# A fused two-model kernel on one core: the modulation summed by VectorE in the last feed-forward, bias lines made in layer 0, two norms in one pass

## The chip, the cores and the metric

The kernel runs on one core of a Trainium2 chip. A core has five engines that run their own instruction streams and meet by semaphores: TensorE (matmuls, results in PSUM), VectorE, ScalarE, GpSimd, and SyncE, which issues the DMAs here. The metric is the device time in microseconds of one execution of the whole program.

## The reference

```python
def first_block(x, ...):                      # DEPTH = 2, S = 512, D = 1024, all float32
    for l in range(DEPTH):
        h = rms_norm(x, norm1[l]); proj = h @ w_in[l]
        ...                                   # four kinds of attention of four heads each
        x = x + mixed @ w_out[l]
        h2 = rms_norm(x, norm2[l])
        x = x + jnp.square(jax.nn.relu(h2 @ w_up[l])) @ w_down[l]
    return rms_norm(x, final_norm)

def second_block(x, c, norm_g, w_ada, b_ada, w_in, ..., rel_bias, final_g):
    mod = c @ w_ada[0] + b_ada[0]             # c: 1 x 1024, w_ada: 1024 x 3072
    shift, scale, gate = jnp.split(mod, 3, axis=-1)
    h = rmsnorm(x, norm_g[0]) * (1.0 + scale[:, None]) + shift[:, None]
    proj = h @ w_in[0]                        # 1024 x 8192
    ...                                       # bias = rel_bias[bucket of the distance], 24 heads
    outs = [dilated_window_attention(q, k, v, dil, win // dil, bias_g) for three groups of eight heads]
    ...                                       # merge of the groups, a pooling branch, gates
    x = x + gate[:, None] * (merged @ w_out[0])
    return rmsnorm(x, final_g)
```

The output of first_block is the input x of second_block. A norm divides each row by the root of its mean square plus 1e-6 and multiplies by a gain.

## The kernel before

X (512 rows as four tiles of 128, 1024 columns) stays in SBUF. A float32 product is made of three passes: each operand is split into a high part, which TensorE multiplies exactly, and a low part, and L1637, L1638 and L1639 (the helper `three`) multiply high by high, high by low and low by high. A product of 512 columns is a *job*: four PSUM banks, G, one for each row tile, in two halves of 512 rows of weights each, so 96 matmuls, which are all of one half before those of the other. Each half's weights are a *piece*: SP loads it into one of four slots of `raw`, ScalarE copies it to `w_hi` (L1144 in the first model, L525 in the second), and GpSimd subtracts in two instructions to `w_lo` (L1107). w_hi and w_lo have two slots, so a piece can be split as soon as the half two before it is done. All engines work strictly in the order in which their streams are written; nothing but that order and the semaphores decides.

A layer has six projection jobs (index, A, C, B, D, V), the index scores with a search for the top keys, the attention, two output jobs and the feed-forward: four groups, each with two jobs up and two down. In a group VectorE squares and splits the hidden rows (L1620 to L1622), and for each bank of a down job adds to X (L1603), which frees the bank. These groups are a hardware loop on every engine. The norm of the feed-forward is not applied before it but as a factor of this addition.

The second block begins with a stage of its own (`second_scalar`, `second_vector`, `second_tensor`, from L525, L614 and L845). TensorE computes the modulation in six dense jobs: the 1 x 1024 vector c, spread over 128 rows as cb_hi and cb_lo, times 512 columns of w_ada each. All 128 rows of each result are the same. VectorE takes the rows to h_full (L641), TensorE turns them into columns, and VectorE adds b_ada (L651). In the same loop TensorE makes 24 bias lines (one for each head: the one-hot table `hot` of distances times a head's row of rel_bias, L874), which ScalarE stores 128 rows wide in `stage` (L536). They go to memory in one 4.6 MB store, from which skewed loads make the bias tiles. Meanwhile the first model's last norm is applied to X (squares L1152, root L1157, rows L633), the second model's norm is then taken of the new X in the same way (L1152, L1376), the rows are turned, scaled and shifted (L560) and split (L668, L669), and the first product of w_in_2 starts once all eight column tiles are split.

## Time and profile before

| | us |
|---|---|
| median of 3 runs | 2209.36 |
| lowest and highest run | 2195.4, 2210.68 |
| the profiled execution | 2206.09 |
| its span, first to last instruction | 2204.1 |
| busy: TensorE, VectorE, ScalarE, GpSimd | 1976.2, 957.9, 666.0, 798.4 |

The profile is of one execution. Its mean granted TensorE clock was 0.932 of full speed. In the rows below, PE is TensorE, PEld its weight loads, DVE VectorE, ACT ScalarE, POOL GpSimd and SPq the DMA queue of SyncE. L numbers are lines of the kernel; many operations share the line of a helper. `a<-b,c` reads: a is written from b and c. A bracket at the end of a row is the time for which the engine stood idle before it and what released it. Busy times of TensorE overlap, since one matmul is issued while the one before still drains: at full clock a 512-column matmul lasts 0.39 to 0.40 us and starts 0.23 us after the one before. The second block's first stage lies between about 1470 and 1565 us.

### The profile page before, as it was taken

How to read it: one execution, taken by the hardware profiler on the slowest of the kernel's cores; microseconds unless marked ns; L12 is line 12 of the kernel's file. 1: busy time of each engine (PE TensorE's matmuls, PEld its weight loads, DVE VectorE, ACT ScalarE, POOL GpSimd, SP SyncE). 2: the span in 40 equal slices, each digit the busy share in tenths (PEclk: the TensorE clock that was granted, in tenths of full speed). 3: DMA queues.
4: the chain of work that ended last, by engine and by line, in shares of the span. 5: the costliest groups of instructions: out<-in, count | busy, mean ns of one | idle time of the engine just before them, and what ended most of it. 6: DMA issues, size and time to landing. Idle time of an engine off the chain costs nothing.

```text
span 2204.1 us, 23720 instructions
## 1 busy us (share of the span) xinstructions
PE 1976.2 (90%) x9164; PEld 1568.6 (71%) x9168; DVE 957.9 (43%) x1704; ACT 666.0 (30%) x1167; POOL 798.4 (36%) x366
## 2 busy tenths in 40 slices
PE   7789889999999977988999999988889898788986
PEld 6556557878778855755777878765688786666765
DVE  3567842322323346875241422332111223756773
ACT  4333443312212342344231222234332323221211
POOL 4223233344444431323334444457331322132441
PEclk9888999999999988989999999998898888898998
DMA  6212001222222331200122222334631132031210
GB/s 191 75 39 77 1 1 58 96 92 91 84 95 79 89 108 39 69 9 1 41 94 95 95 79 94 113 98 153 229 96 37 40 116 77 2 100 57 96 58 38
DMA packets 109520, 170.89 MB, mean 78 GB/s; under 512 B 21724, under 2 KB 39388, under 8 KB 109309
## 3 DMA queue, kind: packets, MB, share of 16 engines
q1 hardware_dynamic: 109436, 169.76, 24.1%
q8 instruction: 55, 0.90, 0.2%
q14 instruction: 29, 0.23, 0.0%
HBM read 161.85 MB, written 7.90 MB: 77 GB/s over the span
## 4 chain that ended last, share of the span: by engine, by line
PE 62%; issue 14%; DVE 10%; POOL 10%; ACT 3%; SPq 1%; DMA 0%; DVEq 0%; POOLq 0%; ACTq 0%
PE G L1637 17%; PE G L1639 16%; PE G L1638 16%; POOL w_lo L1107 9%; PE S L1794 2%; PE G L1831 2%; PE G L1811 1%; PE G L921 1%; DVE qkv L771 1%; PE S L1679 1%; ACT prob L577 1%; POOL prob L1116 1%; PE G L907 1%; DVE select L1462 1%; PE G L1778 1%
## 5 line engine op out<-in xcount | busy, mean ns | idle before, releaser
L1107 POOL TENSOR_TENSOR w_lo<-raw,w_hi 128x1024 fp32r<-128x1024 f32 x296 | 721.0, 2458 | 1214.4 <-ACT w_hi L1144 753.0
L1637 PE MATMUL G<-h_hi,w_hi 128*128 128x512 f32 x896 | 361.0, 403 | 22.9 <-DVE qkv L772 11.6
L1144 ACT ACTIVATE w_hi<-raw 128x2048 fp32r<-128x2048 f32 x96 | 183.7, 1914 | 609.6 <-PE G L1639 609.6
L1638 PE MATMUL G<-h_lo,w_hi 128*128 128x512 f32 x896 | 358.6, 400 | 0.0
L1639 PE MATMUL G<-h_hi,w_lo 128*128 128x512 f32 x896 | 358.0, 400 | 0.0
L1637 PE MATMUL G<-w_hi,h_hi 128*128 128x512 f32 (+2 forms) x704 | 275.5, 391 | 17.0 <-DVE h_lo L777 8.2
L1639 PE MATMUL G<-w_hi,h_lo 128*128 128x512 f32 (+2 forms) x704 | 271.9, 386 | 0.0
L1638 PE MATMUL G<-w_lo,h_hi 128*128 128x512 f32 (+2 forms) x704 | 271.9, 386 | 0.0
L1637 PEld LDWEIGHTS G<-h_hi,w_hi 128*128 128x128 f32 x896 | 171.3, 191 | 68.3 <-DVE qkv L772 12.1
L1638 PE MATMUL G<-w_lo,u_hi 128*128 128x512 f32 x512 | 202.1, 395 | 0.0
L1639 PE MATMUL G<-w_hi,u_lo 128*128 128x512 f32 x512 | 202.1, 395 | 0.0
L1637 PE MATMUL G<-w_hi,u_hi 128*128 128x512 f32 x512 | 202.1, 395 | 0.0
L1639 PEld LDWEIGHTS G<-h_hi,w_lo 128*128 128x128 f32 x896 | 171.1, 191 | 42.1
L1638 PEld LDWEIGHTS G<-h_lo,w_hi 128*128 128x128 f32 x896 | 171.2, 191 | 41.4 <-issue 0.4
L525 ACT ACTIVATE w_hi<-raw 128x2048 fp32r<-128x2048 f32 x50 | 95.6, 1912 | 303.9 <-PE G L1639 287.7
L1603 DVE SCALAR_TENSOR_TENSOR X<-G,inv_square,X 128x512 f32<-128x512 f32 x64 | 48.1, 752 | 293.4 <-PE G L1639 293.4
L1637 PEld LDWEIGHTS G<-w_hi,h_hi 128*128 128x128 f32 x704 | 143.5, 204 | 40.8 <-DVE h_lo L777 8.7
L1638 PEld LDWEIGHTS G<-w_lo,h_hi 128*128 128x128 f32 x704 | 143.6, 204 | 22.0 <-issue 0.5
L1639 PEld LDWEIGHTS G<-w_hi,h_lo 128*128 128x128 f32 x704 | 142.8, 203 | 22.4
L1620 DVE TENSOR_TENSOR square<-relu 128x512 f32<-128x512 f32 x64 | 54.6, 852 | 207.5 <-ACT relu L1337 205.9
L1116 POOL TENSOR_TENSOR prob<-prob,inv_sum 128x256 f32<-128x256 f32 (+2 forms) x64 | 75.0, 1172 | 159.0 <-DVE inv_sum L1548 157.8
L1639 PEld LDWEIGHTS G<-w_hi,u_lo 128*128 128x128 f32 x512 | 96.3, 188 | 22.9
(279 smaller groups left out, 2496.4 us busy)
## 6 DMA issues: line engine op xcount, KB each, us to landing
raw<-in_w_in_dram SPq DMA_DIRECT2D x40, 1024.0 KB, 5.2
raw<-in_w_up_dram SPq DMA_DIRECT2D x32, 1024.0 KB, 5.3
raw<-in_w_down_dram SPq DMA_DIRECT2D x32, 1024.0 KB, 5.0
raw<-in_w_out_dram SPq DMA_DIRECT2D x12, 1024.0 KB, 5.0
raw<-in_w_ada_dram SPq DMA_DIRECT2D x12, 1024.0 KB, 5.1
skew_scratch<-stage SPq DMA_DIRECT2D x1, 4608.0 KB, 14.9
raw<-in_w_in_dram SPq DMA_DIRECT2D x8, 512.0 KB, 4.3
raw<-in_w_in_dram SPq DMA_DIRECT2D x4, 832.0 KB, 4.5
```

What stands on the lines that cost most here:

```text
L525: act.activation(w_hi[:, c % SPLIT_SLOTS], raw[:, c % RAW_SLOTS], ACT.Copy).then_inc(high_ready, 1)
L577: ins = act.activation(part[:, n, :], part[:, n, :], ACT.Exp, bias=head_neg[:, g, m, h:h + 1], accum_out=head_sum[:, g, m, h:h + 1])
L1107: ins = pool.tensor_tensor(w_lo[:, c % SPLIT_SLOTS, part], raw[:, c % RAW_SLOTS, part], w_hi[:, c % SPLIT_SLOTS, part].bitcast(F32), ALU.s ...
L1116: pool.tensor_tensor(part, part, inverse, ALU.mult).then_inc(prob_scaled, 1)
L1144: act.activation(w_hi[:, c % SPLIT_SLOTS], raw[:, c % RAW_SLOTS], ACT.Copy).then_inc(high_ready, 1)
L1603: dve.scalar_tensor_tensor(dst, G[:, t, :], factor, dst, ALU.mult, ALU.add).then_inc(bank_drained, 1)
L1620: step.done(dve.tensor_tensor(square[:], relu[:, n % 2, :], relu[:, n % 2, :], ALU.mult))
L1637: pe.matmul(dst, a_hi, b_hi, start=first, stop=False)
L1638: pe.matmul(dst, a_hi, b_lo, start=False, stop=False)
L1639: return pe.matmul(dst, a_lo, b_hi, start=False, stop=last)
L1794: pe.matmul(bank, qkT[at, p % 2, q, P * qt:P * qt + P], qkT[at, p % 2, k, P * tiles[0]:P * (qt + 1)], start=True, stop=False)
L1831: ins = pe.matmul(dst, values(p, e, kb), probT[:, i % 2, e, P * b:P * b + P], start=b == 0, stop=b == len(tiles) - 1)
```

## The change

- The six jobs are gone. SP loads w_ada in four parts of two 128-row tiles (3 MB each), one in each group of the last feed-forward, behind the fifth piece of the group. VectorE multiplies each tile's rows by c's element of that row and adds them to ada_sum (128 x 3072) in passes of 1024 columns, six a group, each before one of the additions to X. TensorE then sums over the rows: 16 matmuls of one column give shift and scale as columns, two with ones on the left give the gate in every row.
- The last feed-forward is written out on VectorE and SP in place of the loop. The second model's parameters are loaded behind its first group.
- The two norms are one pass. In the last group VectorE also writes X times the final gain (to xn2) for each half tile, ScalarE squares X and xn2 in halves (16 squares), and VectorE works out both factors together. Scaling X itself is moved behind the split of h. The transposes of the first four column tiles follow the row tiles, and the first product waits for its columns by halves.
- The bias lines are made in layer 0, behind the index job: three matmuls give 8 rows each, VectorE copies them to `line`, SP stores them (36 KB), and a DMA from memory to memory spreads each line 128 times, behind the last piece of the output weights. ScalarE waits for the small store before it writes mla_q, which lies on the same memory.
- In SP's stream the skewed bias loads wait for xn2, and the load of the last gain for the scaled X; both stand between the first and the second product's pieces.

```diff
-                    sp.wait_ge(small_drained, SM2_BIAS + B2_HEADS + PAIR_CREDIT)
-                    sp.dma_start(skew_dram.rearrange("h p u -> p h u"), stage[:]).then_inc(skew_saved, 16)
-                    sp.wait_ge(x_scaled, 1)
-                    sp.dma_start(gain_row[:], A["final_g_2"].unsqueeze(0).broadcast_to([P, D_MODEL])
-                                 ).then_inc(gain2_loaded, 16)
+                    sp.wait_ge(xn2_ready, TT)
                     sp.wait_ge(skew_saved, 16)
                     for g in (1, 2):
                         sp.dma_start(bias_far[:, g - 1], skewed(g * B2_H, B2_H, P, P)).then_inc(bias_loaded, 16)
                     sp.dma_start(bias_near[:], skewed(0, B2_H, 0, 2 * P)).then_inc(bias_loaded, 16)
+                    sp.wait_ge(x_scaled, 1)
+                    sp.dma_start(gain_row[:], A["final_g_2"].unsqueeze(0).broadcast_to([P, D_MODEL])
+                                 ).then_inc(gain2_loaded, 16)
...
-            act.wait_ge(x_scaled, 1)
-            square_sums(xn2)
-            square_roots(DEPTH + 1)
-            ahead(ADA + 1, 1)
-            bias_rows(1)
-            for job in range(2, QKV):
-                ahead(job, 0)
-                ahead(job, 1)
-                bias_rows(job)
-
+            for half in range(2):
+                at = slice(512 * half, 512 * half + 512)
+                for t in range(TT):
+                    act.wait_ge(scaled_ready, TT * half + t + 1)
+                    for n, rows in enumerate((xn2, X)):
+                        k = 2 * (TT * half + t) + n
+                        if k >= 2:
+                            act.wait_ge(half_squared, k - 1)
+                        act.activation(h_full[:, n, :], rows[:, t, at], ACT.Square,
+                                       accum_out=halves[:, half, n, t:t + 1]).then_inc(half_squared, 1)
...
-            for ins in scaled_rows(2 * DEPTH, DEPTH):
-                pass
-            ins.then_inc(x_scaled, 1)
-            dve.wait_ge(x_scaled, 1)
-            take_modulation(0)
-            normal_rows(2 * DEPTH + 1, DEPTH + 1, xn2).then_inc(xn_ready, 1)
-            for job in range(1, QKV):
-                take_modulation(job)
-                if job <= 4:
-                    modulation_columns(job - 1)
-            dve.wait_ge(tr_drained, TR2_NORM + PAIR_CREDIT)
+
+            dve.wait_ge(half_squared, 4 * TT)
+            total = newton2[:]
+            step.done(dve.tensor_tensor(total, halves[:, 0], halves[:, 1], ALU.add))
+            dve.tensor_scalar(var2[:, 1, :], total[:, 1, :], 1.0 / D_MODEL, EPS, ALU.mult, ALU.add)
+            step.done(dve.tensor_scalar(var2[:, 0, :], total[:, 0, :], 1.0 / D_MODEL, None, ALU.mult))
+            step.done(dve.scalar_tensor_tensor(var2[:, 0, :], var2[:, 1, :], EPS, var2[:, 0, :], ALU.mult, ALU.add))
+            dve.engine_nop().then_inc(var_ready, 1)
+            dve.wait_ge(mod_filled, 1)
+            step.done(dve.tensor_tensor(mod[:], S[:, 3, 0:2 * KT], mod_b[:], ALU.add))
             dve.scalar_tensor_tensor(mod[:, KT:2 * KT], mod[:, KT:2 * KT], 1.0, norm_col[:], ALU.add,
                                      ALU.mult).then_inc(mod_ready, 1)
+            dve.wait_ge(std_ready, DEPTH + 1)
+            root(var2[:], root2[:], rstd2[:], newton2[:])
+            for t in range(TT):
+                dve.tensor_scalar(xn2[:, t, :], xn2[:, t, :], rstd2[:, 0, t:t + 1], None, ALU.mult).then_inc(xn2_ready, 1)
+                if t == 0:
+                    for n in range(2):
+                        at = slice(512 * n, 512 * n + 512)
+                        ins = dve.tensor_tensor(gate_row[:, at], S[:, 1 + n, :], gate_row[:, at], ALU.add)
+                    ins.then_inc(mod_taken, 1)
...
+            for t in range(TT):
+                ins = dve.scalar_tensor_tensor(X[:, t, :], X[:, t, :], rstd2[:, 1, t:t + 1], gain_row[:], ALU.mult, ALU.mult)
+            ins.then_inc(x_scaled, 1)
...
-            pe.wait_ge(c_ready, 1)
-            all_drained(ADA)
-            for job in range(QKV):
-                if job >= 4:
-                    all_drained(job - 3)
-                for half in range(2):
-                    pe.wait_ge(low_ready, piece2(job) + half + 1 + RAW_SLOTS)
-                    for kk in range(HALF_K):
-                        k = half * HALF_K + kk
-                        ins = three(G[:, job % 4, :], cb_hi[:, k, :], cb_lo[:, k, :], w_hi[:, half, kk, :],
-                                    w_lo[:, half, kk, :], k == 0, k == KT - 1)
...
+            pe.wait_ge(ada_ready, 1)
+            for k in range(2 * KT):
+                pe.matmul(S[:, 3, k:k + 1], ada_sum[:, P * k:P * k + P], ones[:, 0:1], start=True, stop=True)
+            for n in range(2):
+                at = slice(2 * D_MODEL + 512 * n, 2 * D_MODEL + 512 * n + 512)
+                ins = pe.matmul(S[:, 1 + n, :], ones, ada_sum[:, at], start=True, stop=True)
+            ins.then_inc(mod_filled, 1)
+            pe.wait_ge(tr_drained, TR2_NORM + PAIR_CREDIT)
+            pe.wait_ge(mod_ready, 1)
+            for t in range(TT):
+                pe.wait_ge(xn2_ready, t + 1)
+                for k in range(HALF_K):
+                    if t == 0 and k == 1:
+                        pe.wait_ge(mod_taken, 1)
+                    ins = pe.transpose(S[:, k, P * t:P * t + P], xn2[:, t, P * k:P * k + P], ident)
+                    if t == TT - 1:
+                        ins.then_inc(tr_filled, 1)
+            turn_rows(TR2_NORM, lambda k, t: xn2[:, t, P * k:P * k + P], HALF_K, KT)
...
-                    product(unit2(job), piece2(job), rows if s == 2 else in_columns(h_hi, h_lo))
+                    ready = (lambda half: pe.wait_ge(tr_drained, TR2_NORM + HALF_K * (half + 1) + PAIR_CREDIT)) if job == QKV else None
+                    product(unit2(job), piece2(job), rows if s == 2 else in_columns(h_hi, h_lo), inputs_ready=ready)
...
+                    if c == 3 and l == 0:
+                        sp.dma_start(hot[0:NUM_BUCKETS + 1], c_hot[:, :, :]).then_inc(hot_loaded, 16)
+                        sp.dma_start(rel_row[0:NUM_BUCKETS, :], A["rel_bias_2"]).then_inc(hot_loaded, 16)
+                        sp.dma_start(c_col[:], A["c_2"][0, :].rearrange("(k p) -> p k", p=P),
+                                     allow_slow_non_contiguous=True).then_inc(c_loaded, 16)
+                    if c == 6 and l == 0:
+                        sp.wait_ge(line_ready, 1)
+                        sp.dma_start(line_dram.rearrange("(g h) u -> h g u", h=B2_H), line[0:B2_H]).then_inc(line_saved, 16)
+                    if c == FIRST_GROUP_PIECE - 1 and l == 0:
+                        sp.wait_ge(line_saved, 16)
+                        sp.dma_start(skew_dram, line_dram.unsqueeze(1).broadcast_to([B2_HEADS, P, SKEW])
+                                     ).then_inc(skew_saved, 16)
...
+                        if c == 4 and l == DEPTH - 1:
+                            sp.wait_ge(ada_free, g + 1)
+                            rows = slice(ADA_TILES * g * P, ADA_TILES * (g + 1) * P)
+                            sp.dma_start(w_ada[:], A["w_ada_2"][0, rows, :].rearrange("(k p) n -> p k n", p=P)
+                                         ).then_inc(ada_loaded, 16)
+
+                if l == DEPTH - 1:
+                    for g in range(FFN_GROUPS):
+                        group_loads(g)
+                        if g == 0:
+                            second_params(sp)
+                else:
+                    with sp.Fori(0, FFN_GROUPS) as g:
+                        group_loads(g)
...
+                if l == 0:
+                    act.wait_ge(line_saved, 16)
...
+                if l == 0:
+                    dve.memset(rel_row[NUM_BUCKETS:NUM_BUCKETS + 1, :], NEG).then_inc(rel_ready, 1)
+                    dve.wait_ge(line_filled, 1)
+                    dve.tensor_copy(line[0:B2_H], S[0:B2_H, 0:3, 0:SKEW]).then_inc(line_ready, 1)
...
-                        add_to_x(first, j, inv_square)
+                        for t in range(TT):
+                            if last:
+                                add_modulation(g, TT * j + t)
+                            add_to_x(first, j, inv_square, [t])
+                            if last and g == FFN_GROUPS - 1:
+                                if t == 0 and j == 0:
+                                    dve.wait_ge(b2_loaded, 6 * 16)
+                                dve.wait_ge(bank_drained, first + (t + 1 + UNITS_CREDIT))
+                                at = slice(512 * j, 512 * j + 512)
+                                dve.tensor_tensor(xn2[:, t, at], X[:, t, at], gain_row[:, at], ALU.mult
+                                                  ).then_inc(scaled_ready, 1)
                     step.restart()
...
+                    if n == 0:
+                        dve.wait_ge(ada_loaded, 16 * (g + 1))
+                    if n >= ADA_PARTS:
+                        return
+                    tile, at = n // 3, slice(D_MODEL * (n % 3), D_MODEL * (n % 3) + D_MODEL)
+                    k = ADA_TILES * g + tile
+                    step.done(dve.scalar_tensor_tensor(ada_sum[:, at], w_ada[:, tile, at], c_col[:, k:k + 1], ada_sum[:, at],
+                                                       ALU.mult, ALU.add))
+                    if n == ADA_PARTS - 1:
+                        dve.engine_nop().then_inc(ada_free if g < FFN_GROUPS - 1 else ada_ready, 1)
+
+                if l == DEPTH - 1:
+                    dve.wait_ge(c_loaded, 16)
+                    step.done(dve.memset(ada_sum[:], 0.0))
+                    dve.engine_nop().then_inc(ada_free, 1)
+                    for g in range(FFN_GROUPS):
+                        group(g)
+                else:
+                    with dve.Fori(0, FFN_GROUPS) as g:
+                        group(g)
...
+                if l == 0:
+                    pe.wait_ge(hot_loaded, 32)
+                    pe.wait_ge(rel_ready, 1)
+                    for g in range(3):
+                        ins = pe.matmul(S[0:B2_H, g, 0:SKEW], rel_row[0:NUM_BUCKETS + 1, B2_H * g:B2_H * g + B2_H],
+                                        hot[0:NUM_BUCKETS + 1, g, :], start=True, stop=True)
+                    ins.then_inc(line_filled, 1)
+                    pe.wait_ge(line_ready, 1)
                 project(JOB_A)
```

VectorE, end of the last feed-forward and begin of the second block, before (L256 ends the loop; xn is xn2):

```order
966 L1613 COMPARE_AND_BRANCH
967 L619 CAST cb_hi<-c_col 128x1024
968 L620 TENSOR_TENSOR cb_lo<-c_col,cb_hi 128x1024
969 L622 MEMSET rel_row 1x24
970 L623 COPY rel_wide<-rel_row 33x3072
971 L629 TENSOR_SCALAR var<-sumsq 128x4
972 L1356 RECIPROCAL rstd<-std 128x4
973 L1357 TENSOR_TENSOR newton<-rstd 128x4
974 L1358 TENSOR_TENSOR newton<-newton,var 128x4
975 L1359 TENSOR_SCALAR newton<-newton 128x4
976 L1360 TENSOR_TENSOR rstd<-rstd,newton 128x4
977 L633 SCALAR_TENSOR_TENSOR X<-X,rstd,gain_row 128x1024 x4
```

The same place in the change, from the second down job of the last group on:

```order
1069 L1644 SCALAR_TENSOR_TENSOR ada_sum<-w_ada,c_col,ada_sum 128x1024
1070 L1596 SCALAR_TENSOR_TENSOR X<-G,inv_square,X 128x512
1071 L1632 TENSOR_TENSOR xn_123<-X,gain_row 128x512
1072 L1644 SCALAR_TENSOR_TENSOR ada_sum<-w_ada,c_col,ada_sum 128x1024
1073 L1647 ISA
1074 L1596 SCALAR_TENSOR_TENSOR X<-G,inv_square,X 128x512
1075 L1632 TENSOR_TENSOR xn_123<-X,gain_row 128x512
1076 L1596 SCALAR_TENSOR_TENSOR X<-G,inv_square,X 128x512
1077 L1632 TENSOR_TENSOR xn_123<-X,gain_row 128x512
1078 L1596 SCALAR_TENSOR_TENSOR X<-G,inv_square,X 128x512
1079 L1632 TENSOR_TENSOR xn_123<-X,gain_row 128x512
```

The passes over w_ada and the multiplications by the gain stand between the additions to X; the pass over X for the final norm is no longer ahead of the second norm.

SP's queue at the begin of the second block in the change:

```order
97 L1065 DMA raw<-in_w_up_dram 128x4x512 x4
98 L1065 DMA raw<-in_w_down_dram 128x4x512
99 L1069 DMA w_ada<-in_w_ada_dram 128x2x3072
100 L1065 DMA raw<-in_w_down_dram 128x4x512 x3
101 L482 DMA raw<-in_w_in_dram 128x4x512 x2
102 L488 DMA bias_far<-skew_scratch 128x8x128 x2
103 L489 DMA bias_near<-skew_scratch 128x8x256
104 L491 DMA gain_row<-in_final_g_dram 128x1024
105 L482 DMA raw<-in_w_in_dram 128x4x512 x14
```

The load of w_ada stands in front of three pieces of its group, and the bias and gain loads in front of all pieces from the second product on.

## Rows read from the trace of the kernel before

**Rows 1.** Windows: us, busy of PE, PEld, DVE, ACT, POOL (count), PEclk, DMA share, GB/s
```profile
1381.50:1470.50 89.00, 88.96 (x382) 71.28 (x380) 25.22 (x32) 18.05 (x17) 39.00 (x16) 1.00 0.32 95
1470.50:1565.10 94.60, 72.64 (x241) 48.27 (x241) 42.81 (x52) 51.41 (x64) 66.70 (x26) 0.83 0.47 155
```

**Rows 2.** Timeline, end of the last feed-forward: start us, duration us, instruction [idle before]
```profile
1470.06 0.40 PE L1639 MATMUL G<-w_hi,u_lo 128*128 128x512 f32 x1
...
1470.49 1.91 ACT L1144 ACTIVATE w_hi<-raw 128x2048 fp32r<-128x2048 f32 x1 [9.29 <-PE G L1639]
```

**Rows 3.** Timeline, last column tile and the first product of the second block
```profile
1563.01 0.78 ACT L560 ACTIVATE h_full<-S,mod 128x512 f32<-128x512 f32 x1 [0.29 <-DVE h_lo L669]
...
1563.89 0.42 DVE L668 CAST h_hi<-h_full 128x512 fp32r<-128x512 f32 x1
1564.35 0.69 DVE L669 TENSOR_TENSOR h_lo<-h_full,h_hi 128x512 fp32r<-128x512 f32 x1
...
1565.09 0.80 PE L1637 MATMUL G<-h_hi,w_hi 128*128 128x512 f32 x1 [3.60 <-DVE h_lo L669]
...
1571.49 0.39 PE L1637 MATMUL G<-h_hi,w_hi 128*128 128x512 f32 x1
```

**Rows 4.** Lines, stretch 1470.5 to 1565.1: count | busy us, mean ns | idle before
```profile
L1637 PE MATMUL G<-w_hi,cb_hi 128*128 128x512 f32 x48 | 23.2, 484 | 10.5 <-POOL w_lo L1107 7.8 <-DVE cb_lo L620 2.7
...
L874 PE MATMUL S<-hot,rel_wide 33*128 33x384 f32 x48 | 21.4, 571 | 5.7 <-ACT stage L536 5.7
L633 DVE SCALAR_TENSOR_TENSOR X<-X,rstd,gain_row 128x1024 f32<-128x1024 f32 x4 | 11.2, 2870 | 0.0
```

**Rows 5.** Single lines: count: ns min/median/max, first and last start us
```profile
L1152 ACT ACTIVATE xn<-X x12: 1040/1040/1056, 1472.3 to 2192.1; 128x1024 f32<-128x1024 f32 x12
L1207 ACT ACTIVATE select<-rows_a x8: 402/404/408, 57.9 to 786.8; 128x256 f32<-128x256 f32 x8
L1376 DVE TENSOR_SCALAR xn<-X,rstd x4: 745/749/2834, 1499.9 to 1501.9; 128x1024 f32<-128x1024 f32 x4
L633 DVE SCALAR_TENSOR_TENSOR X<-X,rstd,gain_row x8: 1280/1285/3423, 1480.5 to 2199.4; 128x1024 f32<-128x1024 f32 x8
```

**Rows 6.** Timeline, the norm at the kernel's end
```profile
2194.82 0.18 DVE L1356 RECIPROCAL rstd<-std 128x4 f32<-128x4 f32 x1 [1.27 <-ACT std L1157]
...
2195.83 4.87 DVE L633 SCALAR_TENSOR_TENSOR X<-X,rstd,gain_row 128x1024 f32<-128x1024 f32 x4
```

**Rows 7.** Timeline, GpSimd in the last group of the last feed-forward
```profile
1450.09 4.76 POOL L1107 TENSOR_TENSOR w_lo<-raw,w_hi 128x1024 fp32r<-128x1024 f32 x2 [6.44 <-ACT w_hi L1144]
1461.29 4.76 POOL L1107 TENSOR_TENSOR w_lo<-raw,w_hi 128x1024 fp32r<-128x1024 f32 x2 [6.44 <-ACT w_hi L1144]
```

**Rows 8.** DMA issues, 1400 to 1700: count, KB each, median us to landing
```profile
raw<-in_w_ada_dram SPq DMA_DIRECT2D x12, 1024.0 KB, 5.1
skew_scratch<-stage SPq DMA_DIRECT2D x1, 4608.0 KB, 14.9
...
gain_row<-in_final_g_dram SPq DMA_DIRECT2D x1, 512.0 KB, 15.9
```

**Rows 9.** Timeline, the second product's first piece: issue, and ScalarE that waits for it
```profile
1570.63 72.93 SPq L475 DMA_DIRECT2D raw<-in_w_in_dram  x10
...
1579.97 1.92 ACT L525 ACTIVATE w_hi<-raw 128x2048 fp32r<-128x2048 f32 x1 [16.19 <-DMA raw<-in_w_in_dram]
```

**Rows 10.** Timeline, layer 0: end of the index job, the next, a feed-forward load
```profile
36.38 0.30 PE L1639 MATMUL G<-w_hi,h_lo 128*128 128x296 f32 x1
37.15 0.46 PE L1637 MATMUL G<-w_hi,h_hi 128*128 128x420 f32 x1 [0.47 <-POOL w_lo L1107]
...
352.35 0.38 SPq L1092 DMA_DIRECT2D raw<-in_w_up_dram  x1
```

**Rows 11.** Timeline, two waits of TensorE in the modulation's jobs
```profile
1473.16 0.50 PE L1637 MATMUL G<-w_hi,cb_hi 128*128 128x512 f32 x1 [2.70 <-DVE cb_lo L620]
...
1494.01 0.80 PE L1637 MATMUL G<-w_hi,cb_hi 128*128 128x512 f32 x1 [3.28 <-POOL w_lo L1107]
```

135 lines of the change are left out of this document (44 added, 91 removed).

## Prediction

> **What bounds the kernel now.** I read the windows first, to see which engine fills the stretches that the change touches. In the last group of the last feed-forward TensorE is busy 88.96 of 89.0 us at the full clock, VectorE 25.22, ScalarE 18.05, GpSimd 39.00 [rows 1]. There TensorE sets the time and VectorE has room. Between the feed-forward's last matmul (1470.46 [rows 2]) and the first matmul of the second block's products (1565.09 [rows 3]) lie 94.6 us, in which VectorE is busy 42.8, ScalarE 51.4 and GpSimd 66.7 [rows 1]. The view by lines says what fills them: three lines of 48 matmuls each for the modulation (23.2 us the first), 48 matmuls of the bias lines (21.4), and four VectorE passes over X that took 11.2 [rows 4]. Since TensorE resumes useful work only at the end of this stretch, its length is on the path from end to end. After 1565.09 the program is the same but for what stands below, and I take its time over.
>
> **1. The stretch is replaced by one norm chain.** I rebuild it from the last matmul.
> - ScalarE is in order, and the feed-forward's last piece of weights waits for the last matmul. So its w_hi comes first, 1470.49 plus 1.91, and only then the squares [rows 2]. To 1472.4.
> - 16 squares of 128x512 with their sums. No row has that shape; by the line through 0.404 us for 256 columns and 1.04 for 1024 [rows 5] one takes 0.62, and 16 take 9.9. Bounds: 16 x 0.404 = 6.5 and 16 x 1.04 = 16.6. I take 9.9, since both ends are the same operation. To 1482.3. Only the last tile's operands come late, about 2 us after the last matmul, and ScalarE reaches them last.
> - The table load before the root is seen bare at the kernel's end: VectorE waits 1.27 us for it [rows 6]. The four small VectorE operations fit beside it (4 x 0.2). Then root, 0.2, and five small operations, 1.0 (2194.82 to 2195.83 [rows 6]). To 1484.9.
> - Four scalings at 0.75 [rows 5] and two gate additions at 0.69: 4.4. GpSimd has no piece left to split by then, so I take the short value; the 2.83 in the same row is an operation beside GpSimd, and is the upper bound for one or two of them (+4). To 1489.3.
> - Transposes of the last tile to the first bank 0.3, ScalarE's column 0.8, then four columns at 1.06 each (0.42 + 0.69, less overlap), then four transposes, 0.5 [rows 3]. To 1495.2. The new wait by halves lets the product start here; columns 5 to 8 end 4.3 us later, well inside the first half (over 11 us).
> - Hand-overs not counted: 0.3. Start 1495.5, and TensorE starts at half clock as it did (0.80 us at 1565.09, 0.39 only from 1571.49 [rows 3]).
> The 94.6 us become 25.0: **-69.6 us**. The 16 one-column and two 512-column matmuls for the modulation run beside the squares: even at 0.8 us each (the longest matmul in rows 3) they are 14 us, and 12 lie free; at the 0.57 mean of the 384-column rows [rows 4] they are 10. Hidden, with a bound of +2.
>
> **2. VectorE's share in the last feed-forward.** 24 passes of 128x1024 over w_ada, 6 a group, and in the last group 8 multiplications by the gain. The nearest operation is the pass over X: 1.28 us alone, up to 3.42 beside GpSimd [rows 5]. A group's VectorE time rises by 6 x 1.28 = 7.7 us (20.5 at worst) from 25 in 89. They stand between the additions that free the product banks. A half of a product takes 11.2 us (GpSimd's pieces, one for each half, stand that far apart [rows 7]), a tile of it 2.8; so banks fill 2.8 us apart, and the next product comes to the last bank three tiles, 8.4 us, after it filled. With one pass held by GpSimd (3.42) and two free, the last addition starts about when it did; in the last group with the gain, some 3 us late. 8.4 covers that. GpSimd for its part takes 4.76 us a piece [rows 7], and w_hi (1.91 [rows 2]) comes before it, so a piece has 11.2 - 2.0 - 4.76 = 4.4 us to spare. If two passes get in front of its two instructions it is 2.6 late. **0 us**, and if the cover went, each piece would cost the excess over 4.4.
> The row shows that the two engines hold each other up: four passes took 11.2 us [rows 4] instead of 5.1. The Trainium skill (SBUF — State Buffer, "SBUF: two separate sides") says that a VectorE operation with two SBUF inputs and a GpSimd operation take turns at a port pair, each holding it for its whole instruction. By that rule passes spread through the feed-forward would each cost GpSimd their own 1.28, and the trace agrees in direction; the sum stays, because 2.6 is under 4.4, and what more would do is the second rival.
>
> **3. Loads.** Each group's w_ada (3 MB) stands in front of raw loads on SP's queue. 1 MB lands in 5.1 us, 4.6 MB in 14.9 [rows 8], so 3 MB takes 10 to 16. A raw piece is asked for four pieces ahead, about 3.4 x 11.2 = 38 us before ScalarE wants it, less its own 5: 33 us of room. **0.** The wait for ada_free holds only SP, whose next pieces have the same room, and so have the parameter loads behind the first group.
> After the norm SP holds the second product's pieces until X is scaled. Columns done at 1498.9, four passes at 1.28 to 1504.0, issue to 1505, landing 5.3 to 9.3 us later (the same load took 1570.63 to 1579.97 behind other transfers [rows 9]): 1510 to 1514. The first half of the product ends 14.1 us after its start, 1509.6, the next piece is needed at 1520.8, and 1.9 + 4.76 go before: it must land by 1514.1. **0**, but with 0 to 4 us to spare.
>
> **4. Bias lines in layer 0.** Before, TensorE went from the index job (last matmul 36.38) to the next at 37.15, released by GpSimd [rows 10]. Now three matmuls (1.2 to 1.7 us by the 0.57 mean [rows 4]), a VectorE copy of 1152 columns from PSUM (twice the 0.75 of 512 columns, about 1.4) and two hand-overs stand between: restart at about 39.6. **+2.4 us**, bounds 0.8 and 5. All that follows in the layer hangs on TensorE, so I let it stay. A wait of 2.70 us was followed by a matmul of 0.50, one of 3.28 by one of 0.80 [rows 11]; the half clock that began there would cost up to 6 us, if it came.
> SP's line store waits for a copy that ends before its next load is due. The memory-to-memory spread, 4.6 MB like the store that took 14.9 us [rows 8], lies in front of the feed-forward's first loads; those are wanted only after the attention, and SP asks for the next at 352.35 [rows 10]. Even five times 14.9 is hidden. In the second block the 4.6 MB store and the ScalarE wait on it vanish; no engine waited on it visibly, 0.
>
> **Sum.** -69.6 + 2.4 = -67.2. The profiled execution took 2206.09 us (span 2204.1), so 2138.9; the median of the runs is 3.3 higher, which gives 2142.2. I forecast **2141 us**.
>
> **Rivals.**
> - *The second product's weights come late.* SP waits for x_scaled, so if the load lands as late as gain_row did (15.9 us [rows 8]) TensorE stands for 7 us. For: the spare is 0 to 4 us. Against: the skewed bias loads, which crowded the queue before, are then done. 2148. 12%.
> - *VectorE and GpSimd lock each other in the last feed-forward.* This one ends slower than before. If each of the 24 passes and 8 multiplications took 3.42 us and all of it came through to TensorE, it would add 109 us: 2139 + 109 = 2248. It decides when a piece takes GpSimd over 9.1 us, or an addition comes over 8.4 us late. Against: GpSimd is free 6.4 of every 11.2 us there, and VectorE 64 of 89. 3%. In part, with 0.5 to 1.5 us on each of the 32, it gives 2155 to 2187: 8%.
> - *The norm chain is longer*: squares at the upper bound (+6.7), scalings held (+4), layer 0 at half clock after its wait (+6): 2150 to 2156. 12%.
> - *The change does not take the stretch away*: if the pieces behind it were late anyhow (GpSimd was busy 66.7 us in it), the product would wait for them. Against: pieces 0 and 1 are split before and directly after the last matmul. 2175 or more; 2%.
>
> **Numbers.** The forecast (2129 to 2149: bounds of the squares, layer 0, and half the spread of the runs, 8 us) has 63%. The range takes in the late weights and the long norm: **2126 to 2160**. A measurement tells 1% (22 us) from no change. Under 2187 lie all but the full lock and a part of the last rival: faster 0.95, same 0.02, slower 0.03.
>
> **What would show it.** Between the feed-forward's last matmul and the first product 23 to 30 us instead of 94.6; in it 16 squares of about 0.62 us behind one w_hi. Last feed-forward: groups of 89 us, TensorE still at 1.00, passes of 1.28 with some to 3.4, GpSimd pieces up to 7.4. Layer 0: a wait of 3 us at 36.5, released by VectorE. Second product: w_hi released by TensorE or, within 4 us, by the load. I am wrong if groups of the last feed-forward are over 92 us, if squares cost over 1 us, or if TensorE waits over 4 us at the second product.

## The result, and the profile after

| | before | changed |
|---|---|---|
| median, us | 2206.8 (4 runs) | 2144.8 (4 runs) |
| lowest and highest run | 2195.4, 2210.68 | 2143.09, 2147.4 |
| ratio, 95% interval | | 0.9728 (0.969 to 0.9767) |
| span of the profiled execution | 2204.1 | 2145.4 |
| busy: TensorE, VectorE, ScalarE, GpSimd | 1976.2, 957.9, 666.0, 798.4 | 1922.4, 1000.7, 633.3, 750.4 |

The change makes the kernel 2.7% faster. The forecast was 2141 us. The two medians of before differ by 2.6 us because this one has a run more. I read the new profile at the places that the prediction named.

**The stretch.** The timeline of the changed kernel behind the last feed-forward (start, duration, engine, line; the rows in between repeat the pattern):

```profile
1479.80 0.40 PE L1667 MATMUL G<-w_hi,u_lo 128*128 128x512 f32 x1
...
1480.24 1.91 ACT L1131 ACTIVATE w_hi<-raw 128x2048 fp32r<-128x2048 f32 x1 [9.28 <-PE G L1667]
...
1482.05 0.61 ACT L542 ACTIVATE h_full<-xn 128x512 f32<-128x512 f32 x1
...
1491.96 1.28 ACT L545 ACT_TABLE_LOAD   x1
...
1493.25 0.21 ACT L545 ACTIVATE root<-var 128x8 f32<-128x8 f32 x1
1493.49 0.20 DVE L1345 RECIPROCAL rstd<-root 128x8 f32<-128x8 f32 x1 [0.47 <-ACT root L545]
...
1494.54 0.75 DVE L629 TENSOR_SCALAR xn<-xn,rstd 128x1024 f32<-128x1024 f32 x1
1495.21 1.28 DVE L633 TENSOR_TENSOR gate_row<-S,gate_row 128x512 f32<-128x512 f32 x2
...
1496.41 2.07 DVE L629 TENSOR_SCALAR xn<-xn,rstd 128x1024 f32<-128x1024 f32 x3
...
1499.49 0.78 ACT L551 ACTIVATE h_full<-S,mod 128x512 f32<-128x512 f32 x1 [6.03 <-PE S L840]
...
1505.21 0.48 PE L1665 MATMUL G<-h_hi,w_hi 128*128 128x512 f32 x1
1505.53 0.39 PE L1666 MATMUL G<-h_lo,w_hi 128*128 128x512 f32 x1
1505.76 0.40 PE L1667 MATMUL G<-h_hi,w_lo 128*128 128x512 f32 x1
```

The last matmul of the feed-forward ends at 1480.20 and the first product starts at 1505.21: 25.0 us instead of the 94.6 of [rows 2, 3]. ScalarE's copy, 16 squares between 1482.05 and 1491.95, table load, root and the small operations follow each other as they were laid out. One thing is otherwise: the matmuls take 0.48 and 0.39 us from the start. Before, the first took 0.80 us and the next ones 0.63 (from 1565.68 on), and 0.39 came only after 6.4 us [rows 3].

The same two stretches as windows (length, then busy time and count of TensorE, its loads, VectorE, ScalarE, GpSimd; granted clock, DMA share, GB/s), to set against [rows 1]:

```profile
1391.20:1480.20 89.00, 89.00 (x385) 71.65 (x383) 50.48 (x44) 18.05 (x16) 41.35 (x16) 1.00 0.25 89
1480.30:1505.70 25.40, 14.18 (x69) 10.23 (x69) 12.33 (x30) 17.69 (x41) 4.67 (x2) 0.60 0.26 71
```

The last feed-forward group is still TensorE's, 89.00 of 89.0 us, though VectorE works 50.5 us in it where it worked 25.2. Its passes over w_ada and the four transfers, as the view by tile has them (24 passes; shortest, median and longest in ns):

```profile
L1644 DVE SCALAR_TENSOR_TENSOR ada_sum<-w_ada,c_col,ada_sum x24: 1274/1938/3430, 1165.7 to 1473.9; 128x1024 f32<-128x1024 f32 x24
...
DMA to landing us min/median/max: 11.2/12.1/12.8
```

**Layer 0.** TensorE behind the index job, to set against [rows 10], where the next job began at 37.15:

```profile
36.36 2.10 PE L1738 MATMUL S<-hot,rel_row 33*8 33x384 f32 x6
...
39.90 0.46 PE L1665 MATMUL G<-w_hi,h_hi 128*128 128x420 f32 x1 [1.44 <-DVE line L1410]
```

The three matmuls are six records (x6): the trace has two records for each float32 matmul, as the 24 bias lines were 48 records in [rows 4].

**The second product's weights.** SP, ScalarE and TensorE in the changed kernel, to set against [rows 9]:

```profile
1514.10 3.79 SPq L482 DMA_DIRECT2D raw<-in_w_in_dram  x4
...
1521.40 1.91 ACT L527 ACTIVATE w_hi<-raw 128x2048 fp32r<-128x2048 f32 x1 [13.76 <-DMA raw<-in_w_in_dram]
...
1523.39 4.74 POOL L1094 TENSOR_TENSOR w_lo<-raw,w_hi 128x1024 fp32r<-128x1024 f32 x2 [36.50 <-ACT w_hi L527]
...
1528.18 0.50 PE L1665 MATMUL G<-h_hi,w_hi 128*128 128x512 f32 x1 [0.34 <-POOL w_lo L1094]
```

ScalarE, released by the load, starts its copy at 1521.40, and the piece is ready half a microsecond too late: the product's last matmul starts at 1527.45, and the next would have followed at 1527.68, not 1528.18.

**Where the time went.** ScalarE copies one piece of weights after another through the whole program, so the starts of these copies are milestones that both kernels share. Changed kernel less before: +4.4 us at the fifth copy (behind the first half of job A of layer 0), +5.7 where layer 1 starts, +9.0 after layer 1's attention, +9.8 at the end of the last feed-forward, -59.9 at the first product (1505.21 less 1565.09), -59.1 at the last copy, -58.7 in the span. So the stretch gave 69.6 us, as forecast, and 9.8 us were lost ahead of it, where 2.4 were forecast.

### The profile page after: what moved, and what is told of

Its sections match the earlier page's. It is cut to its first block, busy times and chain, and to the rows that moved or that the text cites. A ratio compares the mean times of both kernels' runs of the same rounds, so it can differ in the third digit from the quotient of the medians.

```text
span 2145.4 us, 23192 instructions
## 1 busy us (share of the span) xinstructions
PE 1922.4 (90%) x9002; PEld 1525.6 (71%) x9002; DVE 1000.7 (47%) x1725; ACT 633.3 (30%) x1146; POOL 750.4 (35%) x342
## 4 chain that ended last, share of the span: by engine, by line
PE 62%; issue 15%; DVE 10%; POOL 9%; ACT 3%; SPq 1%; DMA 0%; DVEq 0%; POOLq 0%; ACTq 0%
PE G L1665 17%; PE G L1667 16%; PE G L1666 16%; POOL w_lo L1094 8%; PE S L1830 2%; PE G L1867 2%; PE G L1847 1%; PE G L881 1%; DVE qkv L743 1%; ACT prob L566 1%; POOL prob L1103 1%; PE S L855 1%; PE S L1707 1%; DVE select L1455 1%; PE G L1814 1%
## 5 line engine op out<-in xcount | busy, mean ns | idle before, releaser
L1094 POOL TENSOR_TENSOR w_lo<-raw,w_hi 128x1024 fp32r<-128x1024 f32 x272 | 673.0, 2496 | 1200.0 <-ACT w_hi L1131 745.5
L1131 ACT ACTIVATE w_hi<-raw 128x2048 fp32r<-128x2048 f32 x96 | 183.6, 1913 | 617.2 <-PE G L1667 617.2
L527 ACT ACTIVATE w_hi<-raw 128x2048 fp32r<-128x2048 f32 x38 | 72.6, 1911 | 275.3 <-PE G L1667 261.5
L1666 PEld LDWEIGHTS G<-w_lo,u_hi 128*128 128x128 f32 x512 | 96.1, 188 | 25.1
## 6 DMA issues: line engine op xcount, KB each, us to landing
w_ada<-in_w_ada_dram SPq DMA_DIRECT2D x4, 3072.0 KB, 12.1
```

What stands on the lines that cost most here:

```text
L527: act.activation(w_hi[:, c % SPLIT_SLOTS], raw[:, c % RAW_SLOTS], ACT.Copy).then_inc(high_ready, 1)
L1094: ins = pool.tensor_tensor(w_lo[:, c % SPLIT_SLOTS, part], raw[:, c % RAW_SLOTS, part], w_hi[:, c % SPLIT_SLOTS, part].bitcast(F32), ALU.s ...
L1131: act.activation(w_hi[:, c % SPLIT_SLOTS], raw[:, c % RAW_SLOTS], ACT.Copy).then_inc(high_ready, 1)
L1666: pe.matmul(dst, a_hi, b_lo, start=False, stop=False)
```

## The experiments

Three questions were open. What makes up the 69.6 us and what still stands in the 25.0? Are VectorE's passes hidden, and how far from the edge? And what are the 9.8 us lost ahead of the stretch, of which 4.4 arose at the new wait?

### The wait for the bias lines put later

```diff
                     ins.then_inc(line_filled, 1)
-                    pe.wait_ge(line_ready, 1)
                 project(JOB_A)
+                if l == 0:
+                    pe.wait_ge(line_ready, 1)
```

> TensorE's wait for VectorE's copy of the bias lines stands behind job A, not before it; nothing else is changed. The changed kernel started job A at 39.90 us against 37.15 before, its first half ran at 0.55 us a matmul, and behind it everything was 4.35 us later than before. Theory: the wait makes both, 1.4 to 1.9 us of standing and about 1.6 us of half clock after it. So job A starts near 38.1, its matmuls take 0.40 us from the start, the granted clock of 36 to 48 us is 1.00 as before the change, and ScalarE's copies from there on come 3 to 3.6 us sooner than in the changed kernel; total 2138 to 2143 us against 2144.8. Rival: the three small float32 matmuls bring the clock down themselves. Then job A starts near 38.1 and still runs at 0.55 us a matmul for some 4 us, and only 1.8 us come back.

Measured: median 2141.44 us (2140.79 to 2142.76), ratio to before 0.9719 (0.9701 to 0.9736). From the start of the index job's last matmul to the fifth copy it took 10.20 us before (36.38 to 46.58), 14.80 in the changed kernel (36.13 to 50.93) and 11.69 here (36.88 to 48.57). So 3.1 us of the 4.6 came back, as the theory had it. What is left, 1.5 us, I put down to the three small matmuls, the only thing that still stands between the two jobs. The windows 36 to 42 and 42 to 48 us of the changed kernel:

```profile
36.00:42.00 6.00, 4.56 (x18) 2.66 (x17) 3.47 (x6) 2.31 (x2) 3.83 (x2) 0.89 0.67 174
42.00:48.00 6.00, 6.00 (x28) 5.83 (x27) 5.90 (x12) 0.00 (x0) 3.35 (x2) 0.83 0.25 53
```

and with the wait put later:

```profile
36.00:42.00 6.00, 6.00 (x30) 4.21 (x29) 2.73 (x6) 2.39 (x3) 3.83 (x2) 1.00 0.54 131
42.00:48.00 6.00, 6.00 (x34) 5.94 (x33) 5.90 (x9) 0.00 (x0) 4.17 (x2) 1.00 0.23 69
```

In the last column but two the clock is 0.89 and 0.83 with the wait, 1.00 and 1.00 without. The rival, that the small matmuls themselves bring the clock down, has this against it: they are still there. Over all runs of this study the same piece took 11.7 us in the three kernels with the wait put later, 14.7 to 14.8 us in seven of the nine profiles that had the wait, and 13.2 and 13.3 us in the other two, at a clock of 1.00 throughout. Since full clock also came twice with the wait, three profiles without it speak for the wait as the cause but don't prove it. In these profiles the wait costs 1.5 us always and 1.5 to 1.6 more when the clock falls behind it.

### The bias lines alone

The kernel before, with this one part of the change. Taken out of the second block's first stage:

```diff
-                for h in range(4 * job, 4 * job + 4):
-                    pe.wait_ge(small_drained, SM2_BIAS + h + 1)
-                    pe.matmul(S[:, h % 2, 0:SKEW], rel_wide[0:NUM_BUCKETS + 1, h, :], hot[0:NUM_BUCKETS + 1, h // B2_H, :],
-                              start=True, stop=True).then_inc(small_filled, 1)
...
-                    sp.dma_start(skew_dram.rearrange("h p u -> p h u"), stage[:]).then_inc(skew_saved, 16)
```

> The kernel before with one part of the change alone: the bias lines are made in layer 0 and spread in memory, their 24 matmuls, 24 ScalarE stores and the 4.6 MB store of the second block's first stage are gone; the six dense modulation jobs and both norms stay. Theory: the stretch between the last feed-forward and the first product (94.6 us) follows a chain in which the bias matmuls stood for 7.3% and ScalarE's stores for 1.2%, with VectorE's wait before the first of them (2.7 us) not theirs; so 7 to 10 us of the 94.6 go, layer 0 costs 4.35 us, and 3 to 6 us are left: 2201 to 2204 against 2206.8. Rival A: all of the bias matmuls' time (21.4 us) was on the path: stretch 73, total 2189. Rival B: GpSimd's 12 pieces (66.7 us) bound the stretch and none of it was: stretch 94 to 95, total 2211.

Measured: 2197.35 us (2189.7 to 2204.53, 10 runs) against 2204.38, ratio 0.9974 (0.9955 to 0.9994). The first product started at 1548.64, 84.7 us after the last matmul (1463.96), so 9.95 us of the stretch were the bias lines', at the upper end of what was expected. Neither rival holds: not the whole 21.4 us, and not none. (VectorE's copy that prepared these matmuls, rel_wide, 3.72 us, went with them; the 9.95 us are those of both.) In layer 0 it had the same wait as the changed kernel, but at a clock of 1.00, and paid 3.0 us (13.20 against 10.20). 9.95 less 3.0 is 6.9; the medians differ by 7.0 where 3 to 6 were expected, since layer 0 was taken at 4.35, and the interval, 0.06% to 0.45%, is 1 to 10 us.

### The two norms apart

```diff
-                            if last and g == FFN_GROUPS - 1:
...
-                                dve.tensor_tensor(xn2[:, t, at], X[:, t, at], gain_row[:, at], ALU.mult
-                                                  ).then_inc(scaled_ready, 1)
...
+            square_sums(xn2, lambda t: act.wait_ge(bank_drained, UNIT0 + t + 1))
+            square_roots(DEPTH)
+            act.wait_ge(x_scaled, 1)
+            square_sums(xn2)
+            square_roots(DEPTH + 1)
```

> The two norms one after the other again, in the otherwise changed kernel: no multiplication by the gain in the last group; behind the last matmul ScalarE's copy (1.9 us), four whole squares (4.2), table load, root and the small operations (2.7), VectorE's four passes over X (5.1), four squares of the new X (4.2), root again (2.7), and from the first scaling on as in the changed kernel (10.7). Theory: 31.5 us, bounds 30 and 35 (passes beside GpSimd), instead of 25.0, and SP's load for the second product is no longer late (-0.3 us); total +6 us over the changed kernel, 2148 to 2153 with the clock's own differences. So of the 69.6 us that the stretch lost, one pass for the two norms brought only 5 to 10, the bias lines about 10 (84.7 instead of 94.6 us where they alone were moved), and the six dense jobs the other 50 to 55. Rival: both norms' chains had been hidden behind the modulation jobs before and come fully into the open now, VectorE's passes slowed to 2.8 us each as before: 37 to 42 us, total over 2156.

Measured: the stretch was 30.23 us (1474.42 to 1504.65), inside the bounds and 1.3 under the sum. The median, 2144.22 us (2140.38 to 2147.48, ratio 0.9731, 0.9708 to 0.9754), was that of the changed kernel, 0.6 under it: 5.2 us seemed to be missing. So both were run once more, side by side on one chip.

> The two norms apart once more, unaltered. Its stretch was 30.2 us against 25.0, but its median, 2144.2, was that of the changed kernel, 2144.8. Theory: the 5.2 us are real, and the first profile's second block, 594.7 us from the first product to the last piece against 601.2, drew a higher clock (its first group's attention 66.6 us at 0.90 against 72.5 at 0.81). Then beside the changed kernel on the same chip the median is 2 to 6 us above the changed kernel's, with the stretch 30.2 again and the second block at 598 to 602. Rival: something that the one-pass form adds later pays the 5 us back (scaling X behind the first product's operands, 5 us of VectorE; SP's late load, 0.3), the second block stays at 595 to 597, and the medians are within 1 us.

> The changed kernel once more, unaltered, beside the two others here. Theory: what differed in the stages whose code no kernel touched follows TensorE's granted clock, which comes out otherwise from one execution to the next, and is no property of a kernel. In the changed kernel's first profile layer 1's attention took 147.8 us at 0.88, in seven other kernels with the same code 143.3 to 144.8 at 0.93 to 0.91. Then the same kernel gives another length here, most likely 143.3 to 145.0 at 0.93 to 0.91, and its span is 2140 to 2146. Rival: 147.8 at 0.88 again, so it belongs to this kernel. Median 2141 to 2147 either way.

Measured: the norms apart 2148.14 us (2141.38 to 2148.83), the changed kernel 2143.07 (2140.26 to 2147.53). The medians are 5.1 us apart, the stretches 30.23 and 25.27. The ranges of the runs overlap, so the medians alone would not prove it; the stretch, the same to 0.01 us in both profiles, does. In the first profile the second block had drawn a better clock. The windows of its first group's attention there:

```profile
1561.20:1627.80 66.60, 58.26 (x308) 52.04 (x308) 20.03 (x32) 24.26 (x77) 14.18 (x6) 0.90 0.17 50
```

and in the second profile of the same kernel:

```profile
1562.30:1633.30 71.00, 62.67 (x308) 56.06 (x308) 20.02 (x32) 24.26 (x77) 14.17 (x6) 0.83 0.15 47
```

VectorE, ScalarE and GpSimd do the same work in the same time. The granted clock is 0.90 in one and 0.83 in the other, and the stage is 4.4 us longer.

The repeated profile of the changed kernel settles the loss ahead of the stretch too. Layer 1's attention in the changed kernel's first profile:

```profile
932.20:1080.00 147.80, 125.40 (x782) 87.08 (x783) 87.16 (x213) 62.16 (x200) 42.14 (x34) 0.88 0.03 8
```

and in its second:

```profile
929.30:1072.70 143.40, 119.01 (x780) 84.13 (x783) 87.03 (x213) 62.15 (x200) 42.14 (x34) 0.93 0.03 8
```

At the end of the last feed-forward the second profile stood 2.4 us behind the kernel before (1472.93 less 1470.49), not 9.8, and its span was 2139.7, 64.4 under before. The rival, that 147.8 us belongs to this kernel, falls. (The kernel without the passes, below, had 144.8 at 0.91.)

### The passes left out, twice, three times

```diff
-                    step.done(dve.scalar_tensor_tensor(ada_sum[:, at], w_ada[:, tile, at], c_col[:, k:k + 1], ada_sum[:, at],
-                                                       ALU.mult, ALU.add))
+                    for _ in range(3):
+                        step.done(dve.scalar_tensor_tensor(ada_sum[:, at], w_ada[:, tile, at], c_col[:, k:k + 1],
+                                                           ada_sum[:, at], ALU.mult, ALU.add))
```

> VectorE's 24 passes over w_ada are left out (the modulation is then b_ada alone); the loads of w_ada, the hand-overs and everything else stay. Theory: they are hidden, so the last feed-forward takes what it took in the changed kernel (its four groups 364.9 us from ScalarE's first copy for them to its last) and before (364.7): within 0.5 us of 364.8, and the stretch behind it 25.0 to 25.3 us. Rival: they hold GpSimd up and this already costs something: 1 us or more less. VectorE's busy time in a group falls from about 38 us to 26 to 28. A second reading: layer 1's attention, whose code is the same in all these kernels, took 147.8 us in the changed kernel at a granted clock of 0.88 and 143.3 at 0.93 with the wait moved. If clock and length go together by chance from one execution to the next, it will lie here between 143 and 148 with a clock between 0.93 and 0.88 that fits; if the length came from something else in the changed kernel it is 147.8 again.

> Each pass over w_ada twice (modulation twice what it should be). With three passes TensorE waited 19.8 us for VectorE's additions and the four groups took 387.2 us instead of 364.9. Theory: four additions with two passes each before them take 4 x (2 x 1.5 + 0.8) = 15 us against 8.4 in which the banks fill, so the last is 6.8 us late, inside the room of 8.4 us: the four groups stay at 365 to 367 us, and the total at 2139 to 2147. Rival: the room is smaller than I counted (the addition itself and the hand-over come out of it), and a part comes through: 370 to 378 us.

> Each of VectorE's 24 passes over w_ada runs three times (the modulation is three times what it should be). Theory of the prediction: the passes are hidden as long as the last addition of a down job comes less than 8.4 us after its bank is filled. With three passes of 1.3 to 1.9 us before each of the four additions of a group's first down job, the four take 4 x (4.8 + 0.9) = 23 us where the banks fill in 8.4, so the last addition is some 14 us late, 6 beyond the room; the second down job has only two such additions and catches up in part. So a group of the last feed-forward goes from 89 us to 93 to 98 us and TensorE waits for VectorE's additions; in all 15 to 35 us over the changed kernel, 2160 to 2180. Rival A (the cover is deeper than I counted): groups stay at 89 us, 2145. Rival B (VectorE and GpSimd lock each other): GpSimd's pieces go from 4.8 to 6.0 us to over 9 us and TensorE waits for w_lo; groups over 100 us, over 2190.

From ScalarE's first copy for the four groups of the last feed-forward to the first one behind them:

| passes | four groups, us | total, us |
|---|---|---|
| kernel before | 364.75 | 2206.8 |
| none | 364.94 | 2142.24 (1 run) |
| one (the change) | 364.92 | 2144.8 |
| two | 369.16 | 2146.56 (1 run) |
| three | 387.17 | 2168.26 (2 runs; ratio 0.984, 0.9817 to 0.9863) |

(By these copies the first group takes 92.3 us and each of the others 90.9 in the changed kernel; the 89.0 of the windows is measured from product to product.) The passes of the change are hidden entirely: without them the groups take the same to 0.02 us. With three, each group was 4.6 to 7.4 us longer (95.5 to 98.3 us) and the total 2168, as expected. What TensorE waits for, in the three-pass kernel between 1100 and 1600 us (total, times, longest):

```profile
PE G L1666 <- DVE X L1596: 19.8, 11, 4.3
PE S L840 <- DVE xn L629: 6.6, 1, 6.6
```

The second row is the stretch behind the feed-forward. Three of the eleven waits, 3.1 us, are in the changed kernel too; the other eight are new. TensorE waits for VectorE's additions, which is what the theory named, and never for GpSimd's w_lo: the lock of the two engines doesn't decide. The timeline of VectorE in the first group shows how (three passes, one addition, and so on):

```profile
1173.86 0.75 DVE L1596 SCALAR_TENSOR_TENSOR X<-G,inv_square,X 128x512 f32<-128x512 f32 x1 [3.08 <-PE G L1668]
1174.53 6.61 DVE L1645 SCALAR_TENSOR_TENSOR ada_sum<-w_ada,c_col,ada_sum 128x1024 f32<-128x1024 f32 x3
1181.17 0.75 DVE L1596 SCALAR_TENSOR_TENSOR X<-G,inv_square,X 128x512 f32<-128x512 f32 x1
1181.84 5.94 DVE L1645 SCALAR_TENSOR_TENSOR ada_sum<-w_ada,c_col,ada_sum 128x1024 f32<-128x1024 f32 x3
1187.82 0.75 DVE L1596 SCALAR_TENSOR_TENSOR X<-G,inv_square,X 128x512 f32<-128x512 f32 x1
1188.48 5.26 DVE L1645 SCALAR_TENSOR_TENSOR ada_sum<-w_ada,c_col,ada_sum 128x1024 f32<-128x1024 f32 x3
1193.77 0.75 DVE L1596 SCALAR_TENSOR_TENSOR X<-G,inv_square,X 128x512 f32<-128x512 f32 x1
```

The first bank was taken at 1173.86 and the fourth at 1193.77, 19.9 us later, where the banks fill in 8.4.

Two passes were expected to be free (365 to 367 us) and were not, by 4.2 us. All of it arose in the last group (95.1 us); the three others took what they took in the changed kernel. Only there the multiplications by the gain stand between the additions as well, which the expectation had left out. The fourth addition of its first down job began at 1461.88, 18.3 us after the first (1443.60), so 9.9 us after its bank was filled. In the three other groups it came 14.6 us after the first, 6.2 us after its bank, and held nothing up. TensorE in the last group:

```profile
1459.89 0.40 PE L1668 MATMUL G<-w_hi,u_lo 128*128 128x512 f32 x1
1462.69 0.50 PE L1666 MATMUL G<-w_hi,u_hi 128*128 128x512 f32 x1 [2.40 <-DVE X L1596]
...
1464.19 0.63 PE L1668 MATMUL G<-w_hi,u_lo 128*128 128x512 f32 x1
...
1467.14 0.40 PE L1666 MATMUL G<-w_hi,u_hi 128*128 128x512 f32 x1
```

The next matmul would have come at 1460.12 and came at 1462.69, 2.6 us late. The twelve from there on took 4.45 us where twelve at full clock take 2.8, mostly because eight of them lasted 0.55 to 0.63 us: 1.65 us more. Together these are the 4.2. So the rival was right in part. The addition itself (0.75 us) and the hand-over come out of the room: to be in time it would have had to start by about 1459.3, 7.3 us after its bank was filled and not 8.4. In the changed kernel the same addition starts 2.5 us after its bank (1449.51 and 1460.37 for the first and the fourth), so some 4.8 us of room are left.

### The squares early

```diff
+                        if l == DEPTH - 1 and isinstance(g, int) and g == FFN_GROUPS - 1 and job == GROUP_JOBS - 1:
+                            half_squares(act)
+                            return
                         ahead_g(job, 1)
...
             act.activation(root2[:], var2[:], ACT.Sqrt).then_inc(std_ready, 1)
+            c = 2 * GROUP_JOBS + 1
+            s = c % RAW_SLOTS
+            split_high(c, (DEPTH - 1) * LAYER_LOADS[s] + ((FFN_GROUPS - 1) * GROUP_LOADS + LOADS_TO_GROUPS[s] + GROUP_LOADS + 16),
+                       (DEPTH - 1) * LAYER_JOBS + (FFN_GROUPS - 1) * GROUP_JOBS + (FFN_JOB + GROUP_JOBS))
```

> In the changed kernel ScalarE's 16 half squares are moved ahead of its copy of the last piece (they now start while the last product runs), that copy goes behind the root, and VectorE works out the root before it adds up the modulation. Theory: in the 25.0 us of the stretch the copy (1.9 us) and all squares but the last two (8.7 us) stood on the path. Now VectorE's last addition and multiplication by the gain end about 2.0 us after the last matmul, two squares 1.3 us, table load and root 1.6, five small operations 1.1, first scaling from about +6.2 us instead of +14.3; the modulation's matmuls are done at about +6.5 and hold nothing for long. Stretch 17 us (16 to 19), total 2136 to 2139. Rival: the modulation's matmuls and its additions become the limit (mod_filled at +6.3, then two additions and two gate additions before the second scaling): stretch 19 to 21, total 2139 to 2141. A second rival: with less standing before it or none, the clock of the first product changes and takes part of it back.

Measured: 2134.45 us (2130.95 to 2139.07), ratio 0.9689 (0.9665 to 0.9713). The stretch was 19.8 us (1475.28 to 1495.08), not 17: the first rival's value. The first scaling did begin 5.5 us after the last matmul, but the shift and scale additions could only start at 1482.29, +7.0 us, when TensorE was done with the gate's matmuls, and the second scaling at 1485.05.

### Everything together, and one step of it moved

The combined kernel has the two edits above, gives the shift and scale columns away ahead of the gate's matmuls, adds the gate behind the four scalings, and loads the second product's weights without a wait for the scaled X:

```diff
-            ins.then_inc(mod_filled, 1)
+                ins = pe.matmul(S[:, 3, k:k + 1], ada_sum[:, P * k:P * k + P], ones[:, 0:1], start=True, stop=True)
+            ins.then_inc(mod_filled, 1)
+            all_drained(QKV)
...
+                ins = pe.matmul(G[:, 2 + n, :], ones, ada_sum[:, at], start=True, stop=True)
+            ins.then_inc(gate_filled, 1)
```

> The best of what was seen, together: TensorE's wait for the bias lines behind job A; the squares ahead of the last piece's copy and the root ahead of the modulation, as in the kernel with early squares (stretch 19.8 us, 2134.5 us); new: the shift and scale columns are handed over before the two matmuls of the gate, whose results go to two product banks and are added behind the four scalings; SP loads the second product's weights without waiting for the scaled X. Theory: the first scaling ends about 6.3 us after the last matmul, the shift and scale additions at +7 (columns ready at +3.9 plus GpSimd beside them), the fourth scaling at +9.6, its transposes +10, ScalarE's column and four columns at 1.06: product from +14.8 to +16 instead of +19.8; no wait for weights in the second product (-0.3 to -0.6 us); layer 0 -1.9 to -3.6 us. Sum -6 to -9 against the early squares: 2126 to 2130 us. Rival: the transposes wait for TensorE's own gate matmuls (done at +7.1) and VectorE's additions go slow beside GpSimd, so the stretch stays at 17 to 19 us: 2130 to 2133.

Measured: 2134.67 us (2134.47 to 2135.2), ratio 0.9684 (0.9667 to 0.9701), the stretch 19.78 us. The forecast of 2126 to 2130 was wrong, and so was the rival of 17 to 19 us. Layer 0 did give 3.1 us (11.69 from the index job's last matmul to the fifth copy, 14.82 in the kernel with early squares), yet the medians of the two kernels are the same: in the profile of early squares the first group's attention of the second block took 67.1 us at a clock of 0.90, here 71.0 at 0.83. Its timeline shows what took the place of the gate's matmuls:

```profile
1477.80 0.76 DVE L633 TENSOR_SCALAR xn<-xn,rstd 128x1024 f32<-128x1024 f32 x1
1478.47 0.17 DVE L636 TENSOR_TENSOR mod<-S,mod_b 128x16 f32<-128x16 f32 x1
1478.60 4.64 POOL L1104 TENSOR_TENSOR w_lo<-raw,w_hi 128x1024 fp32r<-128x1024 f32 x2 [10.15 <-ACT w_hi L1141]
1478.67 2.29 DVE L637 SCALAR_TENSOR_TENSOR mod<-mod,norm_col 128x8 f32<-128x8 f32 x1
1480.88 4.23 DVE L633 TENSOR_SCALAR xn<-xn,rstd 128x1024 f32<-128x1024 f32 x3
```

An operation on eight columns took 2.29 us and three scalings 4.23, all while GpSimd subtracts in two instructions of 2.3 us each. ScalarE's copy had been put in front of the scalings, and that had started GpSimd. So the copy was moved behind the fourth column:

```diff
             for k in range(KT):
                 act.wait_ge(tr_filled, TR2_NORM + k + 1)
...
                                bias=mod[:, k:k + 1]).then_inc(full_ready, 1)
+                if k == HALF_K - 1:
+                    c = 2 * GROUP_JOBS + 1
```

> The combined kernel with one step moved: ScalarE's copy of the first product's second piece goes behind the first four columns, so that GpSimd's 4.6 us on it no longer lie beside VectorE's scalings. In the combined kernel the stretch stayed at 19.8 us: from +6.3 us on, while GpSimd worked on that piece, one small operation took 2.29 us and three scalings 4.23 instead of 0.2 and 2.3. Theory: the two wait for each other. Now the small operation takes about 0.2 us, the scalings 0.75 each, the fourth ends at +9.0, gate additions to +10.4, columns from there 1.1 each: product at +14.7 to +15.5; the second piece is ready about 7 to 9.5 us after the product's start, before it is wanted at 11.2. So 4 to 5 us less than the combined kernel's 2134.7: 2129 to 2131. Rival: these times are VectorE's own behind semaphores, and the stretch stays at 19 to 20 us. Second rival: the piece is now late and TensorE waits 1 to 3 us at the first product's second half, 2131 to 2133.

The same operations now, with the copy and GpSimd's work behind them:

```profile
1479.65 0.75 DVE L634 TENSOR_SCALAR xn<-xn,rstd 128x1024 f32<-128x1024 f32 x1
...
1480.53 0.17 DVE L638 SCALAR_TENSOR_TENSOR mod<-mod,norm_col 128x8 f32<-128x8 f32 x1
1480.61 2.07 DVE L634 TENSOR_SCALAR xn<-xn,rstd 128x1024 f32<-128x1024 f32 x3
...
1482.60 1.28 DVE L643 TENSOR_TENSOR gate_row<-G,gate_row 128x512 f32<-128x512 f32 x2
...
1486.96 1.90 ACT L1142 ACTIVATE w_hi<-raw 128x2048 fp32r<-128x2048 f32 x1
...
1488.94 4.92 POOL L1105 TENSOR_TENSOR w_lo<-raw,w_hi 128x1024 fp32r<-128x1024 f32 x2 [18.63 <-ACT w_hi L1142]
1489.14 0.78 PE L1687 MATMUL G<-h_hi,w_hi 128*128 128x512 f32 x1
```

2.29 us became 0.17 and 4.23 became 2.07. The stretch is 15.0 us as expected (1474.17 to 1489.14) and TensorE does not wait for weights behind it. Measured: 2130.17 us (2126.57 to 2132.88), ratio to before 0.9638 (0.9611 to 0.9665). The changed kernel on the same chip had 0.9704 (0.9676 to 0.9732); the intervals don't meet. This is the fastest version, 13 us under the changed kernel.

## Why the prediction was right, step by step

**1. The stretch: right, and for the reason given.** 94.6 us became 25.0, the very sum. That it is the very sum is in part luck, since the last two terms missed by half a microsecond each and cancelled; the rest held: the copy 1.91, the squares 9.9 (0.61 each, the value read off the line between 256 and 1024 columns), table load 1.28, root and small operations 1.3, scalings and gate 3.9 against 4.4, transposes and columns 6.7 (1498.48 to 1505.21) against 6.2. The runs show what the 69.6 us were: 9.95 the bias lines (84.7 instead of 94.6 with them alone moved), 5.0 to 5.2 the joining of the norms (30.2 against 25.0 and 25.3), and what remains, some 54 us, the six dense jobs. This last is a difference; no kernel had them alone removed. By the chain of work that ended last in the kernel before, from 1470 to 1566, they held the stretch through GpSimd more than through TensorE: GpSimd's splits of pieces (w_lo) have the largest share, 35.8%, and the three matmul lines together 18.6%. One clause failed: that TensorE would start at half clock as it did. It started at 0.48 and 0.39 us a matmul in this profile, at 0.78, 0.63, 0.63 and 0.51 in the second and, in the kernel without the passes, at 0.78 and four times 0.63, both behind a stretch of 25.3 us. From the start of the first product to ScalarE's copy behind the second it took 57.1 us instead of 59.5, a net gain of 2.4, late load included, that was not in the sum.

**2. VectorE's passes: right, 0 us.** 364.92 us for the four groups, 364.94 without passes. The single pass was dearer than I took it, 1.94 us at the median where the sum has 1.28, but the cover was counted from the right thing, the time at which a bank must be free. The room of 8.4 us was tested from the other side: an addition that started 9.9 us after its bank was filled held TensorE up by 2.6 us, not 1.5, so the room is about 7.3. With one pass it is enough: in the last group the fourth addition starts 2.5 us after its bank is filled, where some 3 were forecast. The port rule quoted there (the Trainium skill, SBUF — State Buffer, "SBUF: two separate sides") holds in direction: GpSimd's 64 instructions of the last feed-forward went from a mean of 2462 ns to 2656, 12.4 us in all, and VectorE's 24 passes took 22.6 us more than 24 x 1.28. Where it hurts is not where I looked for it. It decides nothing in the feed-forward, but beside GpSimd the norm chain lengthens by 4.3 us (2.29 + 4.23 against 0.17 + 2.07). The Trainium skill says in the same section (SBUF — State Buffer, "SBUF: two separate sides") that whichever of the two starts first keeps the pair for its whole instruction. The trace agrees: the operation on eight columns began just behind GpSimd's first instruction (1478.67 and 1478.60) and ended at 1480.96, when that one was over (half of 4.64 us, about 1480.92).

**3. Loads: right for w_ada (12.1 us to land, in the range of 10 to 16), and too hopeful by half a microsecond for the second product.** "0, with 0 to 4 us to spare" took the first half of the product as 14.1 us long, since it was to start at half clock. It ran at full clock and was over 2.9 us sooner; the spare was then gone and TensorE stood for about 0.5 us. The late load was one of the rivals, at 7 us; it came, at a fourteenth of that.

**4. Bias lines in layer 0: the mechanism right, the size wrong.** The step said +2.4 us, 0.8 to 5, and half clock for up to 6 "if it came". It cost 3.0 us at full clock (the small matmuls 2.1 us instead of 1.2 to 1.7, because they were priced as three records and are six) and 4.6 with the lower clock, which came in seven profiles of nine. This is the term of the sum that was mis-sized, by 0.6 to 2.2 us.

**The sum.** It said -67.2. The first profile gives a span 58.7 us shorter, the second 64.4. Of the 8.5 us between -67.2 and -58.7, 2.2 are layer 0 and 0.5 the late load. The first product's clock gave 2.9 back (2.4 net of the late load). The rest, 8.7 us, came in stages whose code didn't change: 3.3 in layer 1's attention (147.8 us against 144.5), 2.7 in one attention stage of the second block (80.2 against 77.5, at 0.89 against 0.91), and some 2.7 in smaller steps up and down. The lengths of the first model's attention stages follow the granted clock (below). The second profile of the same kernel lacks the 3.3. The 2.7 are another matter: this stage took 80.2 to 83.9 us in all twelve profiles of kernels with a change, at 0.84 to 0.89, and 77.5 only in the one profile of the kernel before. With a single profile of before it stays open whether that belongs to the change, and so does what sets the clock there.

## What to carry to other kernels

Work that one engine does in the open can go into a stage that another engine bounds, if you count the cover from the moment at which a buffer must be free again, take off the freeing instruction itself, and count every instruction that stands in front of it, the small ones too: twice the passes were free in three groups and not in the one that had eight more multiplications. In a serial chain, look at what each engine starts when it passes by: one copy a few microseconds too early set GpSimd to work beside VectorE and cost all that had been gained. And when two versions differ by less than 10 us in 2140, compare milestones in the traces, stage by stage with the clock beside them, before you believe a median.

## What the runs showed of the hardware

**The clock in stages where TensorE waits often.** Layer 0's and layer 1's attention have the same code in all 13 profiles, and their other engines' busy times are the same to 0.3 us. Their lengths were 141.7 us at a granted clock of 0.94, 143.2 to 143.4 at 0.93, 144.1 at 0.92, 144.5 to 144.8 at 0.91, 146.1 at 0.89 and 147.8 at 0.88. In the second block the two go together less closely: its first group's attention took 72.5 us at 0.79 in the kernel before and 72.5 at 0.81 in the changed one, 71.5 at 0.86 in the second profile of that one, and 66.6 at 0.90 in the norms apart. In the first model the longest came once in layer 1, in the changed kernel's first profile, and once in layer 0, in the fastest kernel of all:

```profile
201.35:349.10 147.75, 125.00 (x779) 87.10 (x782) 87.21 (x213) 62.09 (x199) 42.13 (x34) 0.88 0.06 20
930.60:1074.00 143.40, 119.09 (x780) 84.24 (x783) 87.04 (x213) 62.16 (x200) 42.13 (x34) 0.93 0.03 8
```

**The same wait, two clocks.** Behind the same bare wait of 1.44 us for VectorE's copy TensorE kept full clock in two profiles of nine and lost it for some microseconds in seven. The changed kernel itself did both; its second profile:

```profile
42.00:48.00 6.00, 6.00 (x33) 5.93 (x32) 5.93 (x8) 0.00 (x0) 4.42 (x2) 1.00 0.22 70
```
